# A hybrid decoder layer on one core: parameters loaded as rows of 128 channels, padded sample rows, a first piece split by halves, and matmuls on constants

## The chip, the cores and the metric

The kernel runs on one core of one Trainium2 chip. The metric is the device time of one execution in microseconds; the time before is 1837.62 us, the median of three runs (1835.03 to 1838.05).

## The reference, cut to what matters

One layer of a decoder, for 256 prompt tokens and 8 x 8 sample tokens, D = 2048 channels, all in float32. The part that the change touches is the start:

```
u    = rmsnorm(x, norm_pre_mix)                 # x * rsqrt(mean(x^2) + eps) * w, 320 tokens
proj = u @ w_in                                 # columns: z | xBC | dt | glu
xbc  = silu(conv4(xbc, ssd_conv_w) + ssd_conv_b)
y    = ssd_scan(...) + d_skip * x               # 32 heads
v    = glu_a * sigmoid(glu_b)
vc   = conv31(v, conf_conv_w) + conf_conv_b     # depthwise, over time
conf = silu(layernorm(vc) * conf_norm_w + conf_norm_b)
x    = x + rmsnorm(concat(...) @ w_out, norm_post_mix)
x    = x + rmsnorm(relu(rmsnorm(x, norm_pre_mlp) @ w_up)^2 @ w_down, norm_post_mlp)
```

The per-channel vectors (convolution taps and biases, norm weights, d_skip) come from HBM as rows over 2048 or 3072 channels, and the kernel wants them with the channels on the partitions.

## The kernel before

**Layout.** Activations are held transposed: 16 tiles (NT = 16) of 128 channels by 320 tokens (TOK). A product is exact to about float32 by splitting both sides into a rounded high part (`whi`, `ahi`) and a remainder (`wlo`, `alo`), each as fp32r, and adding three matmuls: hi x hi, hi x lo, lo x hi. Weights come in pieces of 512 channels by 256 columns (512 KB) into four slots `raw[:, slot]`. For each piece ScalarE (ACT) writes `whi` (L662), VectorE (DVE; later in the kernel also GpSimd, POOL) writes `wlo` (L1184, L496), and TensorE (PE) then runs 2 column tiles x 4 channel tiles x 3 = 24 matmuls of 128x128 by 320 columns. Nearly the whole kernel is this stream; every engine's order is written out by hand, and the engines meet only at counting semaphores. A slot is loaded again once its remainder has been taken (`lo_done[slot]`).

**The prologue.** The order of the first 67 us, before the steady stream starts with the loop of L1748 to L1750, is:

1. SyncE (SP) issues the three input loads (`xn`: chunk 2 holds the 64 sample rows, chunks 0 and 1 the 256 prompt rows) and weight pieces s = 0 to 3 (L347), then 14 small loads (L350 to L359) into `prow`, `prow2` and `dsk`: the 31 taps as 31 partitions of 2048 channels, each norm vector and bias as one partition of 2048 channels, the xBC taps and bias as 4 and 1 partitions in two parts. Then pieces s = 4 to 7 and four small pieces s = 8 to 11 (the dt columns), each behind the `lo_done` of its slot. The whole of it is one queue.
2. ACT loads `norm_pre_mix` a second time as one row (`prow0`, L669); PE turns it by 16 transposes of one row (L1757), ACT copies it out as `pmx`.
3. For chunk 2, then 0, then 1: ACT squares and sums the rows (L678) and takes the root (L680), DVE takes the reciprocal (L1199) and scales the rows in place (L1202; chunk 1 in two halves of 1024 columns).
4. PE turns the scaled rows (`turn_rows`, L1763): tiles 0 to 3 ahead of the first piece, in the order chunk 2, chunk 0, tile by tile, then chunk 1. A transpose of chunk 2 loads 64 rows as weights, one of chunks 0 and 1 loads 128. The other twelve tiles are turned one or two at a time between half pieces of matmuls (`TURNS`, `turn_x`), into four PSUM banks that ACT has to empty.
5. ACT rounds piece 0 (`first_split(0)`), then tiles 0 to 3 (`x_hi`, L693), then piece 1, then copies tiles 0 to 3 for later use (`x_keep`, L697); for every later tile it copies and rounds, with the later pieces' `whi` between them. DVE takes piece 0's remainder, the tiles' remainders (`in_lo`, L1208), and so on in the same pattern. Both engines run in order: where ACT waits for piece s to land (`raw_ready`), the tiles behind it wait too.
6. PE's matmuls of a piece (`first_piece`, L1797 to L1799) wait for the whole piece's `lo_done`, and, in the first column tile of every even piece, channel tile by channel tile for `act_ready`. s = 0 to 7 are two column blocks of the glu projection. Then PE turns the parameters (16 transposes of 45 rows at L1812, 8 of 5 rows at L1815), ACT copies them to `par` (channels x parameter) and `sw`, and PE runs the dt pieces s = 8 to 11, twelve matmuls of 32 columns each.
7. Beside it, ACT stores the copied transposed input to HBM (L716, one 2560 KB transfer, once all 16 tiles are copied), and POOL, once PE has used 2, 4 and 6 pieces, loads the convolution states (L454, L457) for use in the stage behind the prologue.

Of the kernel before, what the change touches and what calls it, by code (L numbers as in the profile page):

```python
# [38 lines left out]
TOK = SEQ + NB * DS  # L39
HEADS, HD, GROUPS, STATE = 32, 64, 4, 128  # L40
D_XBC = D + 2 * GROUPS * STATE
# [16 lines left out]

R_CONV, R_CB, R_NW, R_NB, R_SSD, R_PREMIX, R_POSTMIX, R_PREMLP, R_POSTMLP, R_XW, R_XB, R_DSKIP = (
    1, 32, 33, 34, 35, 36, 37, 38, 39, 40, 44, 0)  # L60
NROW = 45

# [42 lines left out]
def build(nc, x_prompt, x_sample, state_ssm, state_ssd_conv, state_conf, w_in, ssd_conv_w, ssd_conv_b,  # L105
# [3 lines left out]
    with ExitStack() as ctx:  # L109
        def sem(name):  # L110
            return ctx.enter_context(nc.semaphore(name))
# [31 lines left out]
        sst = place("sst", [NB * XHALO, D_XBC], at=ar + 15360)  # L143
        prow = place("prow", [NROW, D], at=ar + 18432)
        prow2 = place("prow2", [XTAPS + 1, D_XBC - D], at=ar + 20480)

# [56 lines left out]
        pmx = place("pmx", [P, NT], at=own + 1032)  # L203
        prow0 = place("prow0", [1, D], at=2 * NT * TOK + 4096 * 2 + 2048)
        dsk = place("dsk", [1, HEADS], at=sm)
        hw = place("hw", [HEADS, 8, TOK], at=ar + 18432)
# [26 lines left out]


        raw_ready = [sem(f"raw_ready{s}") for s in range(4)]
        hi_done, weights_used = sem("hi_done"), sem("weights_used")
# [11 lines left out]
        x_trans, x_copied, t1_done = sem("x_trans"), sem("x_copied"), sem("t1_done")  # L248
        par_trans, par_copied, par_done = sem("par_trans"), sem("par_copied"), sem("par_done")
        rooted = sem("rooted")  # L250
# [76 lines left out]
        def _(sp):  # L327
# [10 lines left out]
            for s in range(12):  # L338
                if s < 8:
                    kq, col, width = s // 2, (COL_GLU + D, COL_GLU)[s % 2], 256  # L340
                else:
                    kq, col, width = s - 8, COL_DT, HEADS
                if s == 2:
                    sp.wait_ge(x_in[0], 16)
                if s >= 4:
                    sp.wait_ge(lo_done[s % 4], s // 4)
                sp.dma_start(raw[:, s % 4, :, 0:width], in_k[:, 4 * kq:4 * kq + 4, col:col + width]  # L347
                             ).then_inc(raw_ready[s % 4], 16)
                if s == 3:
                    sp.dma_start(prow[R_CONV:R_CONV + TAPS, :], conf_conv_w[0]).then_inc(par_in, 16)  # L350
                    for r, w in ((R_CB, conf_conv_b), (R_NW, conf_norm_w), (R_NB, conf_norm_b), (R_SSD, ssd_norm_w),
                                 (R_PREMIX, norm_pre_mix), (R_POSTMIX, norm_post_mix), (R_PREMLP, norm_pre_mlp),
                                 (R_POSTMLP, norm_post_mlp)):
                        sp.dma_start(prow[r:r + 1, :], w).then_inc(par_in, 16)
                    sp.dma_start(prow[R_XW:R_XW + XTAPS, :], ssd_conv_w[0, :, 0:D]).then_inc(par_in, 16)
                    sp.dma_start(prow[R_XB:R_XB + 1, :], ssd_conv_b[:, 0:D]).then_inc(par_in, 16)
                    sp.dma_start(dsk[:], d_skip).then_inc(dsk_in, 16)
                    sp.dma_start(prow2[0:XTAPS, :], ssd_conv_w[0, :, D:D_XBC]).then_inc(par_in, 16)
                    sp.dma_start(prow2[XTAPS:XTAPS + 1, :], ssd_conv_b[:, D:D_XBC]).then_inc(par_in, 16)  # L359

# [287 lines left out]
        def _(act):  # L648
# [19 lines left out]

            act.dma_start(prow0[:], norm_pre_mix).then_inc(pmx_in, 16)  # L669
            act.wait_ge(consts, 2)  # L670
# [104 lines left out]
            def glu(i):  # L775
                second = isinstance(i, int) and i == 1
                for c in range(8):
# [14 lines left out]
                    if c == (7 if second else 5):  # L792
# [3 lines left out]
            act.wait_ge(par_trans, 1)  # L796
            act.activation(par[:, 0:8, :], ps[:, 5, 0:8 * NROW].rearrange("p (t r) -> p t r", t=8), ACT.Copy)
            act.activation(par[:, 8:16, :], ps[:, 6, 0:8 * NROW].rearrange("p (t r) -> p t r", t=8), ACT.Copy)
            act.activation(sw[:, NT:NX, :], ps[:, 6, 360:400].rearrange("p (t r) -> p t r", t=8), ACT.Copy
                           ).then_inc(par_copied, 1)  # L800
            first_split(10)
            first_split(11)
            act.wait_ge(par_copied, 1)
            act.activation(sw[:, 0:NT, :], par[:, :, R_XW:R_XB + 1], ACT.Copy).then_inc(par_done, 1)
            ahead(Q_GLU, 0, 6)
# [373 lines left out]
        def _(dve):  # L1179
# [13 lines left out]

            dve.sem_inc(conv_turn, 1)
            dve.wait_ge(consts, 3)
            for r, c in enumerate((2, 0, 1)):
# [4 lines left out]
                for lo, hi in ((0, D),) if r < 2 else ((0, D // 2), (D // 2, D)):  # L1201
                    dve.tensor_scalar(xn[0:n, c, lo:hi], xn[0:n, c, lo:hi], ss[0:n, c:c + 1], None, ALU.mult  # L1202
                                      ).then_inc(xs_done, 1)

# [7 lines left out]
            def first_split(s):  # L1212
                split(s // 4, s % 4, 256 if s < 8 else HEADS)

            dve.wait_ge(pmx_done, 1)
# [10 lines left out]
            dve.tensor_copy(prow[R_DSKIP:R_DSKIP + 1, :].rearrange("a (h p) -> a h p", p=HD),  # L1226
                            dsk[:].unsqueeze(2).to_broadcast([1, HEADS, HD])).then_inc(dsk_done, 1)
            first_split(8)
# [510 lines left out]
        def _(pe):  # L1739
# [15 lines left out]
            pe.wait_ge(pmx_in, 16)  # L1755
            for t in range(NT):
                last = pe.transpose(ps[:, 4, 480 + t:481 + t], prow0[:, t * P:(t + 1) * P], ident[0:1, 0:1])  # L1757
            last.then_inc(pmx_trans, 1)
# [26 lines left out]

            def first_piece(s, kq, bank, tiles, by_tile=False):
                slot = s % 4
                pe.wait_ge(lo_done[slot], s // 4 + 1)
                for n in range(tiles):
                    for k in range(4):  # L1790
                        kk = 4 * kq + k
                        if by_tile and n == 0:
# [7 lines left out]
                    if n == tiles - 1:  # L1800
                        last.then_inc(weights_used, 1)
                    for t in TURNS.get((s, n), ()):
                        turn_x(t)
# [4 lines left out]
            pe.wait_ge(par_in, 16 * 13)  # L1808
            pe.wait_ge(dsk_done, 1)
            pe.wait_ge(ahi_done, NT)  # L1810
            for t in range(NT):
                pe.transpose(ps[:, 5 + t // 8, (t % 8) * NROW:(t % 8 + 1) * NROW], prow[:, t * P:(t + 1) * P],  # L1812
                             ident[0:NROW, 0:NROW])
            for t in range(8):
                last = pe.transpose(ps[:, 6, 360 + 5 * t:365 + 5 * t], prow2[:, t * P:(t + 1) * P],  # L1815
                                    ident[0:XTAPS + 1, 0:XTAPS + 1])
            last.then_inc(par_trans, 1)
            for kq in range(4):
# [425 lines left out]
```

## Time and profile before

| What | Value |
|---|---|
| median of three runs | 1837.62 us |
| the profiled execution | 1837.5 us |
| its span, first to last instruction | 1835.9 us |
| PE busy | 1801.5 us (98%), 12683 instructions |
| DVE busy | 1090.9 us (59%) |
| ACT busy | 769.6 us (42%) |
| POOL busy | 455.2 us (25%) |
| mean granted clock of TensorE | 0.991 of full speed |

Busy shares are means over the whole span. PE is the engine that sets the end; the other engines matter where PE waits for them. In a table of stretches a count in brackets is that of the instruction records in the stretch; some matmul records can be missing, so a count is a lower bound. "PEld" is TensorE's weight load, which runs beside the matmul before it; the distance between the starts of two weight loads shows the pace of PE better than the duration of one matmul, since matmuls overlap.

### The profile page before, as it was taken

How to read it: one execution, taken by the hardware profiler on the slowest of the kernel's cores; microseconds unless marked ns; L12 is line 12 of the kernel's file. 1: busy time of each engine (PE TensorE's matmuls, PEld its weight loads, DVE VectorE, ACT ScalarE, POOL GpSimd, SP SyncE). 2: the span in 40 equal slices, each digit the busy share in tenths (PEclk: the TensorE clock that was granted, in tenths of full speed). 3: DMA queues.
4: the chain of work that ended last, by engine and by line, in shares of the span. 5: the costliest groups of instructions: out<-in, count | busy, mean ns of one | idle time of the engine just before them, and what ended most of it. 6: DMA issues, size and time to landing. Idle time of an engine off the chain costs nothing.

```text
span 1835.9 us, 33891 instructions
## 1 busy us (share of the span) xinstructions
PE 1801.5 (98%) x12683; PEld 1766.1 (96%) x12683; DVE 1090.9 (59%) x1989; ACT 769.6 (42%) x1139; POOL 455.2 (25%) x351
## 2 busy tenths in 40 slices
PE   7999999999999999999899999999999999999998
PEld 6999999999998988899899999999999999999998
DVE  4568887999787677765675433444334443444434
ACT  5443435555355555643353333333324333333332
POOL 1477676776661222222100000000000000000121
PEclk9999999999998999999999999999999999999999
DMA  7665554555554554564345445444444454444442
GB/s 204 192 177 151 162 142 141 152 150 151 152 148 138 169 160 152 163 207 140 115 134 158 145 147 160 151 137 156 153 149 138 143 167 149 137 145 160 153 138 81
DMA packets 286420, 278.33 MB, mean 152 GB/s; under 512 B 11405, under 2 KB 283789, under 8 KB 285412
## 3 DMA queue, kind: packets, MB, share of 16 engines
q1 hardware_dynamic: 247542, 246.56, 44.1%
q10 hardware_dynamic: 37138, 23.08, 4.1%
q0 software_dynamic: 1648, 7.43, 1.3%
q8 instruction: 62, 1.02, 0.2%
q14 instruction: 30, 0.24, 0.0%
HBM read 261.26 MB, written 17.22 MB: 152 GB/s over the span
## 4 chain that ended last, share of the span: by engine, by line
PE 94%; DVE 2%; ACT 2%; DMA 1%; issue 1%; DVEq 0%; ACTq 0%
PE ps L1748 28%; PE ps L1750 28%; PE ps L1749 28%; DMA raw<-in_w_in 1%; PE ps L2065 1%; PE ps L2066 1%; PE ps L2067 1%; PE ps L2026 1%; PE ps L2020 1%; PE ps L1994 1%; PE ps L1971 1%; PE ps L1797 0%; PE ps L2031 0%; PE ps L2029 0%; DVE yo L1732 0%
## 5 line engine op out<-in xcount | busy, mean ns | idle before, releaser
L1748 PE MATMUL ps<-ahi,whi 128*128 128x320 f32 x2304 | 720.2, 313 | 1.9 <-DVE alo L1435 1.9
L1750 PE MATMUL ps<-ahi,wlo 128*128 128x320 f32 x2304 | 713.8, 310 | 0.0
L1749 PE MATMUL ps<-alo,whi 128*128 128x320 f32 x2304 | 713.7, 310 | 0.0
L662 ACT ACTIVATE whi<-raw 128x1024 fp32r<-128x1024 f32 (+1 forms) x468 | 480.2, 1048 | 474.5 <-PE ps L1750 386.8
L1184 DVE TENSOR_TENSOR wlo<-raw,whi 128x1024 fp32r<-128x1024 f32 x347 | 428.6, 1259 | 250.6 <-ACT whi L662 247.3
L1748 PEld LDWEIGHTS ps<-ahi,whi 128*128 128x128 f32 x2304 | 434.4, 189 | 3.9 <-DVE alo L1435 2.2
L1749 PEld LDWEIGHTS ps<-alo,whi 128*128 128x128 f32 x2304 | 434.5, 189 | 0.5
L1750 PEld LDWEIGHTS ps<-ahi,wlo 128*128 128x128 f32 x2304 | 434.2, 188 | 0.0
L1748 PE MATMUL ps<-hhi,whi 128*128 128x320 f32 x1016 | 314.3, 309 | 0.0
L1750 PE MATMUL ps<-hhi,wlo 128*128 128x320 f32 x1016 | 313.9, 309 | 0.0
L1749 PE MATMUL ps<-hlo,whi 128*128 128x320 f32 x1016 | 313.9, 309 | 0.0
L496 POOL TENSOR_TENSOR wlo<-raw,whi 128x1024 fp32r<-128x1024 f32 x121 | 289.5, 2414 | 97.9 <-ACT whi L662 97.5
L1329 DVE SCALAR_TENSOR_TENSOR ps<-vx,par,ps 128x256 f32<-128x256 f32 (+1 forms) x928 | 290.9, 382 | 11.0 <-ACT vx L725 9.9
L633 POOL TENSOR_TENSOR sq<-ya 128x640 f32<-128x640 f32 x7 | 14.7, 2099 | 836.3 <-DVE ya L1696 836.3
L1749 PEld LDWEIGHTS ps<-hlo,whi 128*128 128x128 f32 x1016 | 190.7, 188 | 0.0
L1748 PEld LDWEIGHTS ps<-hhi,whi 128*128 128x128 f32 x1016 | 190.7, 188 | 0.0
L1750 PEld LDWEIGHTS ps<-hhi,wlo 128*128 128x128 f32 x1016 | 190.7, 188 | 0.0
L1086 ACT ACTIVATE hs<-rh 128x640 f32<-128x640 f32 x32 | 23.6, 739 | 205.9 <-DVE rh L1661 205.9
L1661 DVE SCALAR_TENSOR_TENSOR rh<-ps,rb 128x640 f32<-128x640 f32 x32 | 26.4, 824 | 135.2 <-PE ps L1750 135.1
L1696 DVE TENSOR_TENSOR ya<-ps,ya 128x640 f32 (+1 forms) x23 | 19.0, 824 | 111.0 <-PE ps L1750 111.0
L1664 DVE TENSOR_TENSOR hlo<-hs,hhi 128x640 f32 (+1 forms) x32 | 26.4, 825 | 56.7 <-ACT hhi L1088 56.7
L1748 PE MATMUL ps<-ghi,whi 128*128 128x320 f32 x192 | 59.3, 309 | 0.0
(298 smaller groups left out, 1648.9 us busy)
## 6 DMA issues: line engine op xcount, KB each, us to landing
raw<-in_w_in SPq DMA_DIRECT2D x144, 512.0 KB, 3.7
raw<-in_w_up SPq DMA_DIRECT2D x128, 512.0 KB, 4.4
raw<-in_w_down SPq DMA_DIRECT2D x128, 512.0 KB, 4.5
raw<-in_w_out SPq DMA_DIRECT2D x64, 512.0 KB, 3.5
h<-in_state_ssm ACTq DMA_DIRECT2D x16, 512.0 KB, 5.2
out<-hout ACTq DMA_DIRECT2D x16, 512.0 KB, 3.2
x_transposed<-xt ACTq DMA_DIRECT2D x1, 2560.0 KB, 10.5
xr<-x_transposed POOLq DMA_DIRECT2D x1, 2560.0 KB, 9.6
```

The costliest lines, as they stand in the source:

```text
L496: pool.tensor_tensor(wlo[:, kq, :, :], raw[:, kq, :, :], whi[:, kq, :, :].bitcast(F32), ALU.subtract).then_inc(lo_done[kq], 1)
L662: act.activation(whi[:, kq, :, 0:width], raw[:, kq, :, 0:width], ACT.Copy).then_inc(hi_done, 1)
L1086: act.activation(hs[:], rh[:], ACT.Square).then_inc(hs_done, 1)
L1184: dve.tensor_tensor(wlo[:, kq, :, 0:width], raw[:, kq, :, 0:width], whi[:, kq, :, 0:width].bitcast(F32), ALU.subtract).then_inc(lo_done[kq ...
L1329: ins = dve.scalar_tensor_tensor(out=acc[s] if k else src[s], in0=src[s], scalar=par[:, j, R_CONV + k:R_CONV + k + 1], in1=acc[s], op0=ALU ...
L1661: dve.scalar_tensor_tensor(out=rh[:], in0=ps[:, bank:bank + 2, 0:TOK], scalar=0.0, in1=rbb, op0=ALU.max, op1=ALU.mult).then_inc(rh_done, 1)
L1664: dve.tensor_tensor(hlo[:, ds(4 * i + 2 * p, 2), :], hs[:], hhi[:, ds(4 * i + 2 * p, 2), :].bitcast(F32), ALU.subtract).then_inc(hid_ready, 1)
L1696: dve.tensor_tensor(m, gemm_bank(p), m, ALU.add).then_inc(read_dve, 1)
L1748: pe.matmul(out, wh, hi[:, kk, :], start=(kk == 0), stop=False)
L1749: pe.matmul(out, wh, lo[:, kk, :], start=False, stop=False)
L1750: last = pe.matmul(out, wl, hi[:, kk, :], start=False, stop=(kk == NT - 1))
L1971: last = pe.transpose(ps[:, 6 + b // 4, (b % 4) * P:(b % 4 + 1) * P], h0[:, j % 2, b, :], ident[:])
```

## The change

All of it lies in the prologue.

- **Small loads.** Each parameter vector of 2048 channels is loaded as 16 partitions of 128 channels (`pvec`, eight vectors on 128 partitions, d_skip among them), the 31 taps as 4 x 124 rows of 128 channels (`pcv`: 124 partitions, four rows each), the xBC taps and bias as 96 + 24 rows (`pssd`), and `norm_pre_mix` for `pmx` as 16 rows (`pmx0`). Eleven loads instead of 14 behind piece 3. PE turns them with 4 + 1 + 1 transposes, and `pmx0` with one. ACT's three copies write `par` and `sw` with the channel tile running fastest in what they read; the fourth copy goes. `par` has 39 parameters per tile instead of 45.
- **Sample rows padded.** DVE clears partitions 64 to 127 of chunk 2 at the start, and every row transpose loads 128 rows; the 64 more output columns lie in the unused part of the bank (TOK is 320, three chunks of 128 are 384).
- **Chunk 1 scaled in other parts.** 512 columns, 512 columns, and 1024 columns; the last part moves behind the remainders of tiles 0 to 3. PE waits for it ahead of tile 8.
- **Piece 0 split by halves.** ACT rounds channel tiles 0 and 1 of piece 0, then activation tile 0, then channel tiles 2 and 3; DVE takes remainders in the same order; PE waits for the first half at the start and for the second half at the third channel tile.
- **Matmuls on constants.** PE runs `keep_warm(n)`: n matmuls of the bf16 identity with the zeroed `cum3` (320 columns) into bank 3: 20 behind the `pmx` transpose, 8 behind chunk 2's row transposes, 4 behind chunk 0's, 4 behind chunk 1's. The row transposes of tiles 0 to 3 run chunk by chunk.

```diff
-                    sp.dma_start(prow[R_CONV:R_CONV + TAPS, :], conf_conv_w[0]).then_inc(par_in, 16)
-                    for r, w in (... eight vectors ...):
-                        sp.dma_start(prow[r:r + 1, :], w).then_inc(par_in, 16)
...
+                    sp.dma_start(pcv[:], conf_conv_w[0].rearrange("r (t p) -> (r t) p", p=P).rearrange(
+                        "(q a) p -> a q p", a=4 * TAPS)).then_inc(par_in, 16)
+                    sp.dma_start(pssd[0:XTAPS * NX, :], ssd_conv_w[0].rearrange("r (t p) -> (r t) p", p=P)
+                                 ).then_inc(par_in, 16)
...
+                        sp.dma_start(pvec[(r - R_VEC) * NT:(r - R_VEC + 1) * NT, :],
+                                     w.rearrange("o (t p) -> (o t) p", p=P)).then_inc(par_in, 16)
...
+            def first_halves(h):                                   # ACT
+                if h == 0:
+                    act.wait_ge(raw_ready[0], 16)
+                act.activation(whi[:, 0, 2 * h:2 * h + 2, :], raw[:, 0, 2 * h:2 * h + 2, :], ACT.Copy
+                               ).then_inc(first_hi if h == 0 else hi_done, 1)
-            first_split(0)
+            first_halves(0)
             for t in range(4):
                 act.wait_ge(x_trans, t + 1)
                 x_hi(t)
+                if t == 0:
+                    first_halves(1)
...
             dve.wait_ge(pmx_done, 1)                               # DVE
-            first_split(0)
-            for t in range(4):
+            first_halves(0)
+            in_lo(0)
+            first_halves(1)
+            for t in range(1, 4):
                 in_lo(t)
+            scale_rows(P, 1, D // 2, D)
             first_split(1)
...
+            def keep_warm(n):                                      # PE
+                for _ in range(n):
+                    pe.matmul(ps[:, 3, 0:TOK], identb[:], cum3[:], start=True, stop=True)
             def turn_rows(t, c):
-                b, lo = 4 + t % 4, (0, P, SEQ)[c]
-                n = P if c < 2 else NB * DS
-                return pe.transpose(ps[:, b, lo:lo + n], xn[0:n, c, t * P:(t + 1) * P], ident[0:n, 0:n])
+                return pe.transpose(ps[:, 4 + t % 4, c * P:(c + 1) * P], xn[:, c, t * P:(t + 1) * P], ident[:])
...
+            keep_warm(20)
             pe.wait_ge(pmx_done, 1)
-            pe.wait_ge(xs_done, 2)
-            for t in range(4):
-                turn_rows(t, 2)
-                turn_rows(t, 0)
-            pe.wait_ge(xs_done, 3)
+            for c, warm in ((2, 8), (0, 4)):
+                pe.wait_ge(xs_done, 2 if c == 2 else 3)
+                for t in range(4):
+                    turn_rows(t, c)
+                keep_warm(warm)
+            pe.wait_ge(xs_done, 4)
             for t in range(4):
                 turn_rows(t, 1).then_inc(x_trans, 1)
-            pe.wait_ge(xs_done, 4)
+            keep_warm(4)
+            pe.wait_ge(xs_done, 5)
...
-            for t in range(NT):
-                pe.transpose(ps[:, 5 + t // 8, (t % 8) * NROW:(t % 8 + 1) * NROW], prow[:, t * P:(t + 1) * P],
-                             ident[0:NROW, 0:NROW])
...
+            for q in range(4):
+                pe.transpose(ps[:, 5, 4 * TAPS * q:4 * TAPS * (q + 1)], pcv[:, q, :], ident[0:4 * TAPS, 0:4 * TAPS])
+            pe.transpose(ps[:, 6, 0:P], pvec[:], ident[:])
+            pe.transpose(ps[:, 6, P:P + (XTAPS + 1) * NX], pssd[:], ident[0:(XTAPS + 1) * NX, 0:(XTAPS + 1) * NX]
+                         ).then_inc(par_trans, 1)
```

## Rows read from the trace of the kernel before

**Rows 1.** Stretches of PE: stretch, length, busy (records), clock, DMA share, GB/s.
```profile
16.56:24.09 7.53, 7.53 (x33) 1.00 0.55 152
24.09:38.33 14.24, 14.24 (x91) 1.00 0.62 159
38.33:47.28 8.95, 6.49 (x31) 0.81 0.61 134
39.50:41.90 2.40, 0.00 (x0) 1.00 0.97 226
58.60:60.35 1.75, 1.75 (x25) 1.00 0.99 218
60.35:67.43 7.08, 7.08 (x52) 1.00 0.88 262
67.43:1835.90 1768.47, 1747.52 (x12355) 0.99 0.49 149
```

**Rows 2.** The chain that ended last, 38 to 45 us: start, duration, what.
```profile
19.32 19.76 DMA raw<-in_w_in
39.10 1.07 ACT whi L662
...
40.19 1.22 DVE wlo L1184
```

**Rows 3.** Timeline of SyncE's queue: start, duration of the issue.
```profile
9.12 1.60 SPq L350 DMA_DIRECT2D prow<-in_conf_conv_w  x1
...
15.82 32.15 SPq L347 DMA_DIRECT2D raw<-in_w_in  x8
```

**Rows 4.** DMA at 12:14, 24.2:26.8, 48:50 (packets, MB, share); issue at 15.8.
```profile
q1 hardware_dynamic: 696, 0.70, 110.2%
...
q1 hardware_dynamic: 9, 0.07, 6.7%
...
q1 hardware_dynamic: 528, 0.07, 20.9%
...
raw<-in_w_in SPq DMA_DIRECT2D x1, 512.0 KB, 18.3
```

**Rows 5.** Timeline 12 to 17 us, three engines: start, duration, idle before.
```profile
13.18 1.06 ACT L662 ACTIVATE whi<-raw 128x1024 fp32r<-128x1024 f32 x1 [0.17 <-ACT sx L680]
13.24 1.42 DVE L1202 TENSOR_SCALAR xn<-xn,ss 128x1024 f32<-128x1024 f32 x2
14.57 1.22 DVE L1184 TENSOR_TENSOR wlo<-raw,whi 128x1024 fp32r<-128x1024 f32 x1
15.30 1.78 ACT L693 ACTIVATE ahi<-ps,pmx 128x320 fp32r<-128x320 f32 x4 [1.06 <-PE ps L1763]
15.86 1.92 DVE L1208 SCALAR_TENSOR_TENSOR alo<-ps,pmx,ahi 128x320 fp32r<-128x320 f32 x4
16.56 0.60 PE L1797 MATMUL ps<-ahi,whi 128*128 128x320 f32 x1 [0.66 <-DVE alo L1208]
```

**Rows 6.** Timeline of TensorE's weight loads around two groups of transposes.
```profile
30.55 0.29 PEld L1763 LDWEIGHTS ps<-ident,xn 128*128 128x128 f32 x2
...
31.21 0.19 PEld L1797 LDWEIGHTS ps<-ahi,whi 128*128 128x128 f32 x1
...
70.64 0.49 PEld L1828 LDWEIGHTS ps<-ident,cst 120*128 120x128 f32 x4
71.09 0.19 PEld L1748 LDWEIGHTS ps<-ahi,whi 128*128 128x128 f32 x1
```

**Rows 7.** Stretches of PE again: two of equal length.
```profile
18.25:21.66 3.41, 3.41 (x13) 1.00 0.41 108
42.14:45.55 3.41, 3.41 (x13) 0.50 0.69 142
```

**Rows 8.** DMA issues, 0 to 70 us: KB each, median us to landing.
```profile
x_transposed<-xt ACTq DMA_DIRECT2D x1, 2560.0 KB, 10.5
cst<-in_state_conformer_conv POOLq DMA_DIRECT2D x2, 960.0 KB, 9.2
```

More of the change, by code:

```diff
@@ L56 @@
 XNEW = XHALO + NB * XHALO
-R_CONV, R_CB, R_NW, R_NB, R_SSD, R_PREMIX, R_POSTMIX, R_PREMLP, R_POSTMLP, R_XW, R_XB, R_DSKIP = (
-    1, 32, 33, 34, 35, 36, 37, 38, 39, 40, 44, 0)
-NROW = 45
+R_CONV, R_VEC = 0, 31
+R_CB, R_NW, R_NB, R_SSD, R_POSTMIX, R_PREMLP, R_DSKIP, R_POSTMLP = range(31, 39)
+NROW = 39
 Q_DT, Q_GLU, Q_XBC, Q_Z, Q_WC, Q_WS, Q_MLP = 0, 1, 17, 29, 37, 45, 53
@@ L143, in build @@
         sst = place("sst", [NB * XHALO, D_XBC], at=ar + 15360)
-        prow = place("prow", [NROW, D], at=ar + 18432)
-        prow2 = place("prow2", [XTAPS + 1, D_XBC - D], at=ar + 20480)
+        pcv = place("pcv", [4 * TAPS, 4, P], at=ar + 18432)
+        pvec = place("pvec", [P, P], at=ar + 18944)
+        pssd = place("pssd", [(XTAPS + 1) * NX, P], at=ar + 19072)
+        pmx0 = place("pmx0", [NT, P], at=ar + 19200)
+        dsk = place("dsk", [P, 2], at=ar + 19328)
         mix = place("mix", [P, NT, TOK], at=ar)
@@ L232, in build @@
         ps = ctx.enter_context(nc.psum_tensor("ps", [P, 8, 512], F32))
+        first_hi, first_lo = sem("first_hi"), sem("first_lo")
         raw_ready = [sem(f"raw_ready{s}") for s in range(4)]
@@ L248, in build @@
         x_trans, x_copied, t1_done = sem("x_trans"), sem("x_copied"), sem("t1_done")
-        par_trans, par_copied, par_done = sem("par_trans"), sem("par_copied"), sem("par_done")
+        par_trans, par_done = sem("par_trans"), sem("par_done")
         rooted = sem("rooted")
@@ L1194, in _, with scale_rows @@
             dve.sem_inc(conv_turn, 1)
+            dve.memset(xn[NB * DS:P, 2, :], 0.0).then_inc(xs_done, 1)
             dve.wait_ge(consts, 3)
+            def scale_rows(n, c, lo, hi):
+                dve.tensor_scalar(xn[0:n, c, lo:hi], xn[0:n, c, lo:hi], ss[0:n, c:c + 1], None, ALU.mult
+                                  ).then_inc(xs_done, 1)
             for r, c in enumerate((2, 0, 1)):
@@ L1200, in _ @@
                 dve.wait_ge(rx_done, r + 1)
-                for lo, hi in ((0, D),) if r < 2 else ((0, D // 2), (D // 2, D)):
-                    dve.tensor_scalar(xn[0:n, c, lo:hi], xn[0:n, c, lo:hi], ss[0:n, c:c + 1], None, ALU.mult
-                                      ).then_inc(xs_done, 1)
+                if r < 2:
+                    scale_rows(n, c, 0, D)
+                else:
+                    scale_rows(n, c, 0, D // 4)
+                    scale_rows(n, c, D // 4, D // 2)
             def in_lo(t):
@@ L1213, in first_split, with first_halves @@
                 split(s // 4, s % 4, 256 if s < 8 else HEADS)
+            def first_halves(h):
+                dve.wait_ge(*((first_hi, 1) if h == 0 else (hi_done, 1)))
+                dve.tensor_tensor(wlo[:, 0, 2 * h:2 * h + 2, :], raw[:, 0, 2 * h:2 * h + 2, :],
+                                  whi[:, 0, 2 * h:2 * h + 2, :].bitcast(F32), ALU.subtract
+                                  ).then_inc(first_lo if h == 0 else lo_done[0], 1)
             dve.wait_ge(pmx_done, 1)
-            first_split(0)
-            for t in range(4):
+            first_halves(0)
+            in_lo(0)
+            first_halves(1)
+            for t in range(1, 4):
                 in_lo(t)
+            scale_rows(P, 1, D // 2, D)
             first_split(1)
@@ L1787, in first_piece @@
                 slot = s % 4
-                pe.wait_ge(lo_done[slot], s // 4 + 1)
+                if s:
+                    pe.wait_ge(lo_done[slot], s // 4 + 1)
+                else:
+                    pe.wait_ge(first_lo, 1)
                 for n in range(tiles):
                     for k in range(4):
+                        if s == 0 and n == 0 and k == 2:
+                            pe.wait_ge(lo_done[slot], 1)
                         kk = 4 * kq + k
@@ L1802, in first_piece @@
                     for t in TURNS.get((s, n), ()):
+                        if t == 8:
+                            pe.wait_ge(xs_done, 6)
                         turn_x(t)
@@ L1807, in _ @@
                     first_piece(2 * kq + p, kq, 2 * p, 2, by_tile=(p == 0))
-            pe.wait_ge(par_in, 16 * 13)
+            pe.wait_ge(par_in, 16 * 10)
             pe.wait_ge(dsk_done, 1)
             pe.wait_ge(ahi_done, NT)
-            for t in range(NT):
-                pe.transpose(ps[:, 5 + t // 8, (t % 8) * NROW:(t % 8 + 1) * NROW], prow[:, t * P:(t + 1) * P],
-                             ident[0:NROW, 0:NROW])
[L1814 to L1817, printed above, removed]
+            for q in range(4):
[3 more added lines that the diff above has]
+                         ).then_inc(par_trans, 1)
             for kq in range(4):
```

36 lines of the change are left out of this document (16 added, 20 removed).

## The prediction

> **What bounds the kernel now.** The page comes first: TensorE (PE) is busy 98% of the span, so only PE's own work, its gaps and its clock count. The table of stretches says where it is less than full [rows 1]: behind 67.43 us there are 1768.47 us with 20.95 us of gaps in all, and the change touches none of that code. So everything is decided ahead of 67.43 us, and there, in order, by the first matmul's start at 16.56 us [rows 5], by the rate of the first pieces, and by a hole from 39.50 to 41.90 us in which PE does nothing. The chain of waits [rows 2] tells what ended the hole: the sixth weight piece (s = 5) takes 19.76 us from issue to landing, ScalarE rounds it at 39.10, VectorE takes the remainder at 40.19, and only behind these two do the activations of tiles 9 to 11 (already turned) come through the same two in-order engines, which ends the hole at 41.90.
>
> Why is a 512 KB transfer 18 to 20 us on its way? SyncE issues the parameter loads from 9.12 us and the fifth piece behind them at 15.82 [rows 3], which takes 18.3 us [rows 4]. The transfers' own records give it away. From 24.2 to 26.8 us the queue runs 9 packets of 8 KB at 6.7% of sixteen DMA engines: 6.7% x 16 = 1.07, one engine always busy and fifteen idle; a packet is 0.067 x 16 x 2.6 / 9 = 0.31 us. These are the taps' 31 rows and the vectors' single rows, and each piece waits for its share on that engine. 31 + 8 + 1 such packets and parts of others are 40 x 0.31 = 12.4 us of private queue, the shares of two pieces beside it.
>
> For the clock I compare [rows 7]: 18.25 to 21.66 us shows the same 13 matmul records in 3.41 us as 42.14 to 45.55, where the granted clock is 0.50. The first is therefore also the lower level (1.2 GHz), whatever its 1.00 says; PE had before it only short work and a pause. It is 3.41 / 13 = 0.26 us from matmul to matmul there, against 7.08 / 48 = 0.1475 us at 2.4 GHz in the 48 matmuls of the dt pieces [rows 1].
>
> **The change part by part.**
>
> *Earlier start, by halves.* Today the chain is: ScalarE's third root, whi of piece 0 at 13.18 (1.06 us), VectorE's two scalings of 1024 columns from 13.24 (1.42 us together), wlo at 14.57 (1.22), ahi from 15.30, alo from 15.86, first matmul 16.56 [rows 5]. New: scaling of 512 columns ends at about 13.75 (half of a 1024 one is 0.36; with a fixed part 0.5), PE turns the four tiles of chunk 1, the first done at 14.2; ScalarE's half whi (0.53 to 0.65) is done at 13.8, ahi(0) 14.2 to 14.75; VectorE scales the second 512 to 14.1, half wlo to 14.75, alo(0) to 15.3. First matmul 15.4: 1.15 us earlier. But the second half of the split now stands on both engines between tile 0 and tile 1, so alo(1) comes at 16.4, alo(2) 16.85, alo(3) 17.3, and the first half piece ends at 17.8 in 2.4 us instead of 12 x 0.1475 = 1.77: 0.65 given back. The scaling of the other 1024 columns sits on VectorE ahead of piece 1's wlo, which ends at 19.2, as now; PE asks for it at 20.6. The next turn waits for ScalarE's copy behind piece 1's whi (about 17.9), 0.1.
>
> *Warm matmuls.* 20 behind the pmx transpose (3.7 to about 9), 8, 4 and 4 between the row transposes, where PE waits for VectorE's scalings anyway (20 x 0.26 = 5.2 us are over by 9, and the first row transposes can't start before chunk 2 is scaled, at 9.7). If they raise the clock in time, the stretch 16.56 to 24.09 (7.53 us: two half pieces, three turns [rows 1]) shrinks to what the same work takes later. 24.09 to 38.33 is six half pieces and six turns, 14.24 / 6 = 2.37 each, so 1.77 + 0.60; two half pieces and three turns are 5.3: gain 2.2. If not, 0.
>
> *Rows padded to 128.* Three transposes with a 64-row one among them take 30.55 to 31.21 = 0.66 us from weight load to weight load, though four of 120 rows take 70.64 to 71.09 = 0.45 [rows 6]: about 0.10 each once the height stays the same, 0.19 extra at each change. All at 128: 0.36. Gain 0.30 a turn, twelve turns: 3.6. Bounds: -0.6 (64 more columns, 0.05 a turn, and the gap stays) to 3.6. I take 3.6, since rows 6 have equal heights without the gap. The padding's memset is VectorE's first work, ahead of all scalings.
>
> *Parameter rows of 128 channels.* 14 loads become 11. The single vectors become 16 rows of 512 B, the taps 124 partitions x 4 x 512 B, the xBC parameters 96 and 24 rows. No row shows a 512 B packet; the nearest are 1 KB ones, 1.102 x 16 x 2 / 696 = 0.051 us, and 128 B ones, 0.209 x 16 x 2 / 528 = 0.013 us [rows 4]. The taps' 496 packets are then 0.4 us over sixteen engines at the one end and 25 us on a single engine at the other. I take few engines, under 6 us: 124 partitions are near the 128 of the pieces, which fill all sixteen, but like 31 they are no multiple of 16. Piece 4 then lands near 22 us, piece 5 (issued near 19.3) near 24, long before the 33 us at which PE wants them. The hole goes, and the low clock that follows it: 38.33 to 47.28 holds two half pieces and two turns, 4.75 us at the usual rate, and took 8.95 [rows 1]: gain 4.2. What is late next: nothing before 48; ScalarE needs two keeps, two roundings and one or two splits per 4.2 us of PE, some 2.5 us.
>
> The Trainium skill (DMA: Bandwidth & Descriptors, the section on why a DMA increments its semaphore by 16) says that a transfer runs on the largest number of engines up to 16 that divides the slowest dimension of both sides. By that rule the 31 rows go to one engine, which the 6.7% above confirm, but the new 124 partitions only to four, not sixteen: an estimate of 124 packets each, at 0.051 us 6.3 us. No row shows the four; the sum holds with either.
>
> *Parameter transposes.* 24 become 6 of 96 to 128 rows: the 1.75 us of 58.60 to 60.35 become about 1.2 (six x 0.10, three changes of height at 0.19). Gain 0.6. ScalarE's copies move as many numbers as now, beside the dt pieces: 0. pmx: 16 transposes become one, in a gap: 0. The d_skip copy gets short, beside PE: 0.
>
> *What moves with it.* PE reaches the dt pieces near 49.5 instead of 60.35. The store of the transposed input (10.5 us [rows 8]) starts some 10 us earlier, and so do, more or less, the conv states' loads: all keep their distance to PE's use, because each hangs on PE's own counters. The store may now overlap the second state load by 2 to 3 us.
>
> **Sum.** 1.15 - 0.65 - 0.1 + 2.2 + 3.6 + 4.2 + 0.6 = 11.0 us. From this I take 0.8 for the clock: warm bursts of 8, 4 and 4 with pauses for VectorE between them are thin, and if the clock falls again at 13 to 16 us, the first 12 to 16 matmuls cost 0.11 us more each, some 1.5, in about half of the executions. Gain 10.2. The profiled execution took 1837.5 us (span 1835.9 and 1.6 around it), the median shown is 1837.62; so 1837.6 - 10.2 = 1827.4.
>
> **Rivals.**
> (a) *The clock doesn't hold.* For it: in rows 7 the level changes late and after long busy stretches. Against: 5 us of gapless matmuls stand ahead of it. Price: 2.2 of the sum lost, and the transposes of chunks 2 and 0 with their bursts at 1.2 GHz push chunk 1 back by 0.5: 11.0 - 0.8 - 2.2 - 0.5 = 7.5, so 1830.
> (b) *The hole stays*, because the pieces behind the parameter loads are still late, by a remnant on a few engines or by the conv state load (9.2 us for 960 KB) that starts earlier. Gain 11.0 - 4.2 - 0.8 = 6.0, 1831.6. Against: pieces wanted at 33 have 10 us of slack.
> (c) *It is given back later*: the store of 2560 KB and the state load meet the weights of the next stage, and PE waits behind the dt pieces. In the present trace these weights land next to that same store without a PE gap. It would have to cost 10 us: within 0.2%, 1837.
> (d) *Slower*: all 496 packets of the taps on one DMA engine at 0.051 us. Piece 4, issued at 15.8, then lands near 15.8 + 25 + 3 = 44; from about 31 on, each us later is a us of PE. Split at 46.8 instead of the 33.2 at which PE wants it, it costs 13.6, and 1.7 for the low clock behind such a hole: 11.0 - 0.8 - 13.6 - 1.7 = -5.1, 1843. It is slower than before from a landing near 40 on. For: the 31-row load does go to one engine. Against: 128-partition loads don't, and packets of 1 KB behind each other may well be faster than on sixteen busy engines.
> (e) *The padding doesn't do what it says*: the extra 0.19 belongs to the switch between modes, not to the height. 3.6 becomes -0.6: gain 6, 1831.6.
>
> **How the numbers follow.** Main case 0.66 (own range 1825.5 to 1829.5); (a) 0.12; (b) 0.06; (e) 0.06; (c) 0.05; (d) 0.03; 0.02 for something unseen, either side. Later in the kernel the clock falls at a few gaps, and where such a fall begins differs from execution to execution; the three runs lie 3 us apart. So the range is 1824.5 to 1832.5. About 0.2% (3.7 us) can be told from no change: faster 0.90, same 0.06, slower 0.04.
>
> **What would show it.** The first matmul on weights at 15 to 16 us and its neighbours 0.147 us apart; three equal transposes in about 0.36 us between half pieces; no gap of PE near 40 us, pieces 4 and 5 landing within 10 us of issue; the parameter transposes at 47 to 49 us in 1.2 us; gaps behind the dt pieces summing to about the present 21 us. I am wrong if the first pieces run at 0.26, if the 64-row gap survives, if a weight piece still takes over 15 us to land, or if a new gap stands behind 49 us.

## The result, and the profile after

The changed kernel takes 1825.12 us in the median of six runs (1823.92 to 1827.0), the kernel before beside it 1837.66. The ratio is 0.9938, 95% interval 0.9928 to 0.9948: 11.4 us faster, between 9.6 and 13.2 (the medians lie 12.5 apart). One of the six runs of the kernel before took 2197.66 us, and the ratio, which compares fast runs, leaves it out. The forecast was 1827.4 in a range of 1824.5 to 1832.5, faster with 0.90. The time lies in that range, and 0.4 us below the main case's own range.

The profiled execution takes 1823.92 us, span 1822.3. First the stretches of TensorE (columns as in [rows 1]), the same work where the same work can be named:

```profile
15.52:18.05 2.53, 2.18 (x12) 1.00 0.51 143
18.05:30.11 12.06, 12.06 (x90) 1.00 0.71 211
39.50:41.90 2.40, 2.40 (x19) 1.00 0.91 274
48.18:48.88 0.70, 0.70 (x9) 1.00 1.17 385
48.88:55.90 7.02, 7.02 (x52) 1.00 1.01 287
55.90:1822.30 1766.40, 1743.85 (x12356) 0.99 0.49 149
```

The first line is the first half piece: 2.53 us with 0.35 of gap, at full pace. The third is the place of the old hole: full. The steady loop's first matmul starts at 55.88. Before, it was at 67.27; the 67.43 that stands ahead of the result is the end of the last matmul of the dt pieces. What lies behind the loop's start, code that the change doesn't touch, is 2.3 us shorter (1766.5 instead of 1768.8, by the starts of weight loads).

TensorE's timeline of the start (start, duration, operation, count, and in brackets the idle time before it and what ended it); the constants' matmuls are the bf16 ones:

```profile
3.68 5.51 PE L1790 MATMUL ps<-cum,identb 128*128 128x320 bf16 x20
9.87 0.63 PE L1793 MATMUL ps<-ident,xn 128*128 128x128 f32 x4 [0.67 <-DVE xn L1212]
10.33 1.25 PE L1790 MATMUL ps<-cum,identb 128*128 128x320 bf16 x8
12.67 0.71 PE L1790 MATMUL ps<-cum,identb 128*128 128x320 bf16 x4
15.52 0.39 PE L1835 MATMUL ps<-ahi,whi 128*128 128x320 f32 x1 [0.42 <-DVE alo L1229]
16.55 0.42 PE L1835 MATMUL ps<-ahi,whi 128*128 128x320 f32 x1 [0.35 <-DVE alo L1229]
```

The 20 take 5.2 us at 0.26 each, the four behind chunk 0 take 0.71 with the tail: the pace has doubled by then, and the pauses for VectorE between them don't lose it. The weight loads around a turn and around the parameters, against [rows 6]:

```profile
17.91 0.40 PEld L1793 LDWEIGHTS ps<-ident,xn 128*128 128x128 f32 x3
18.27 0.19 PEld L1835 LDWEIGHTS ps<-ahi,whi 128*128 128x128 f32 x1
...
48.16 0.50 PEld L1852 LDWEIGHTS ps<-ident,pcv 124*128 124x128 f32 x4
48.63 0.14 PEld L1853 LDWEIGHTS ps<-ident,pvec 128*128 128x128 f32 x1
48.73 0.14 PEld L1854 LDWEIGHTS ps<-ident,pssd 120*128 120x128 f32 x1
48.85 0.11 PEld L1835 LDWEIGHTS ps<-ahi,whi 128*32 128x32 f32 x1
```

A turn is 18.27 - 17.91 = 0.36 us instead of 0.66. The six parameter transposes take 48.85 - 48.16 = 0.69 us, 0.11 each, although their heights change among 128, 124 and 120.

SyncE's queue (start and duration of the issue; answers to [rows 3]) and what its transfers took (KB each, us to landing; answers to [rows 4, 8]): piece 4, piece 5, piece 7, the store and the state loads.

```profile
9.23 1.74 SPq L352 DMA_DIRECT2D pcv<-in_conf_conv_w  x1
11.01 5.31 SPq L354 DMA_DIRECT2D pssd<-in_ssd_conv_w  x1
...
20.41 18.60 SPq L349 DMA_DIRECT2D raw<-in_w_in  x8
```

```profile
raw<-in_w_in SPq DMA_DIRECT2D x1, 512.0 KB, 5.1
raw<-in_w_in SPq DMA_DIRECT2D x1, 512.0 KB, 4.9
raw<-in_w_in SPq DMA_DIRECT2D x1, 512.0 KB, 10.5
x_transposed<-xt ACTq DMA_DIRECT2D x1, 2560.0 KB, 10.2
cst<-in_state_conformer_conv POOLq DMA_DIRECT2D x2, 960.0 KB, 8.9
```

Pieces 4 and 5 land 5.1 and 4.9 us after their issue, where they took 18.3 and 19.8. Piece 7, issued just ahead of a state load, still takes 10.5. But one small issue holds SyncE for 5.31 us, and piece 4 is issued at 20.4 where it went out at 15.82 before; I had left it at 15.8. It lands at 25.5 and its half pieces are run from 33.2, so nothing of this shows in TensorE.

Where the 11.3 us come from, by the starts of weight loads of the same half pieces in both traces:

```
                                   before          after          gain
first half piece starts            16.53           15.49          1.04
two half pieces, three turns       16.53-24.09     15.49-20.68    2.37
six half pieces, six turns         24.09-38.33     20.68-33.17    1.75
two half pieces, two turns (hole)  38.33-47.28     33.17-37.33    4.79
up to the parameter transposes     47.28-58.65     37.33-48.16    0.54
parameter transposes               58.65-60.35     48.16-48.85    1.01
dt pieces, to the steady loop      60.35-67.12     48.85-55.85   -0.23
```

### The profile page after: what moved, and what is told of

Read it like the earlier page. It is cut to its first block, busy times and chain, and to the rows that moved or that the text cites. A ratio compares the mean times of both kernels' runs of the same rounds, so it can differ in the third digit from the quotient of the medians.

```text
span 1822.3 us, 33899 instructions
## 1 busy us (share of the span) xinstructions
PE 1793.7 (98%) x12686; PEld 1758.8 (97%) x12686; DVE 1088.4 (60%) x1992; ACT 769.9 (42%) x1139; POOL 457.4 (25%) x351
## 3 DMA queue, kind: packets, MB, share of 16 engines
q8 instruction: 62, 1.02, 0.2%
## 4 chain that ended last, share of the span: by engine, by line
PE 95%; DVE 2%; ACT 1%; issue 1%; DMA 0%; SPq 0%; DVEq 0%; ACTq 0%
PE ps L1778 28%; PE ps L1779 28%; PE ps L1780 28%; PE ps L2103 1%; PE ps L2105 1%; PE ps L2104 1%; PE ps L2064 1%; PE ps L2058 1%; PE ps L1835 1%; PE ps L2032 1%; PE ps L1837 1%; PE ps L1836 1%; PE ps L2009 1%; DMA xn<-in_x_prompt 0%; PE ps L2069 0%
## 5 line engine op out<-in xcount | busy, mean ns | idle before, releaser
L1197 DVE TENSOR_TENSOR wlo<-raw,whi 128x1024 fp32r<-128x1024 f32 x346 | 424.1, 1250 | 245.8 <-ACT whi L666 242.7
## 6 DMA issues: line engine op xcount, KB each, us to landing
x_transposed<-xt ACTq DMA_DIRECT2D x1, 2560.0 KB, 10.2
```

The lines of the kernel that those rows point to most:

```text
L1197: dve.tensor_tensor(wlo[:, kq, :, 0:width], raw[:, kq, :, 0:width], whi[:, kq, :, 0:width].bitcast(F32), ALU.subtract).then_inc(lo_done[kq ...
```

## The experiments

Each was timed beside the kernel before, whose median there was 1836.18 us (e1, e2, e4, e5), 1838.27 (e3, e6, e7, e8) or 1835.11 (e10, e11). "dt" and "loop" are the starts of the first weight load of the dt pieces and of the steady loop in the profiled execution; "root" is when VectorE takes up the last root of the norms (the reciprocal), which the input's arrival moves by up to 0.4 us; "rest" is the span behind the loop's start.

```
                    ratio   95% interval      median   root   dt     loop   rest
before                                        1837.66  13.04  60.35  67.12  1768.8
after               0.9938  0.9928 to 0.9948  1825.12  13.16  48.85  55.85  1766.5
e1_no_warm          0.9947  0.9928 to 0.9966  1827.29  13.02  51.24  58.99  1768.3
e2_short_rows       0.9965  0.9951 to 0.9979  1828.90  13.08  52.22  59.22  1768.0
e3_late_params      1.0031  1.0019 to 1.0044  1842.29  12.99  64.84  73.32  1767.1
e4_whole_piece      0.9944  0.9926 to 0.9962  1824.50  13.07  48.82  55.80  1766.8
e5_params_only      0.9981  0.9972 to 0.9991  1832.09  13.17  54.57  62.15  1765.1
e6_one_engine       0.9973  0.9963 to 0.9983  1832.89  13.13  57.19  64.17  1770.8
e7_only_20          0.9957  0.9942 to 0.9972  1830.31  13.08  49.78  56.77  1769.0
e8_later_quarter    0.9941  0.9924 to 0.9957  1825.82  12.87  48.56  55.54  1766.6
e10_pool_halves     0.9951  0.9938 to 0.9965  1826.94  13.30  48.96  55.92  1769.4
e11_changed_again   0.9944  0.9930 to 0.9957  1825.54  13.16  48.85  55.85  1769.4
```

The rest varies by 5.7 us with no relation to the edits, so dt and loop tell kernels apart more finely than the ratios. Each of them is read from one profiled execution; e11 says how well they repeat. By the ratios alone only e2, e3, e5 and e6 are apart from the changed kernel, the intervals of e1, e4, e7, e8 and e10 overlap its own.

**No matmuls on constants.**

```diff
-                for _ in range(n):
+                for _ in range(0):
```

> The changed kernel without any of the matmuls on constants. Measured by where the steady loop's first matmul stands: 67.43 us in the kernel before, 56.0 in the changed one. Theory (the constants raise the clock): the first matmuls on weights stand 0.26 us apart instead of 0.147 until the clock rises, and the loop starts 2.2 us later, 58.2, between 57 and 59. Rival (the clock would have risen anyway, or the row transposes raise it): 56.0.

The first two half pieces with their three turns take 15.50 to 23.07 = 7.57 us instead of 5.19: 2.38 for the clock, as worked out (2.2). With the root made equal (13.02 against 13.16) it is 2.5 up to the dt pieces. The loop starts 3.14 later, though, and the further 0.75 has another cause. TensorE's first matmul of the loop, and GpSimd's first two remainders there:

```profile
59.02 0.39 PE L1778 MATMUL ps<-ahi,whi 128*128 128x320 f32 x1 [0.63 <-POOL wlo L500]
```

```profile
56.49 4.75 POOL L500 TENSOR_TENSOR wlo<-raw,whi 128x1024 fp32r<-128x1024 f32 x2 [1.63 <-ACT whi L666]
```

and in the changed kernel:

```profile
53.31 4.79 POOL L500 TENSOR_TENSOR wlo<-raw,whi 128x1024 fp32r<-128x1024 f32 x2 [2.30 <-ACT whi L666]
```

The first of the two ends half way, at 58.9 here and at 53.31 + 2.4 = 55.7 in the changed kernel, where TensorE's first matmul of the loop is at 55.88; before, it ended at 65.9 for 67.27. So a cover of 1.4 us has shrunk to 0.2. What GpSimd and ScalarE wait for stands ahead of them in the chain that ended last in e1, the weight piece of the next stage:

```profile
44.30 11.02 DMA raw<-in_w_in
```

It is on its way, beside the store of 2560 KB, for 11.0 us here (and in e5), for 10.2 in the changed kernel and for 9.5 before. Why it differs no run isolates.

**Rows of 64 again.**

```diff
-                return pe.transpose(ps[:, 4 + t % 4, c * P:(c + 1) * P], xn[:, c, t * P:(t + 1) * P], ident[:])
+                n = P if c < 2 else NB * DS
+                return pe.transpose(ps[:, 4 + t % 4, c * P:c * P + n], xn[0:n, c, t * P:(t + 1) * P], ident[0:n, 0:n])
```

> The changed kernel with the sample rows' transposes on 64 rows again. Theory (each change of height costs 0.19 us): twelve turns of 0.66 instead of 0.36 us, loop start 59.6, time 3.6 us longer. Rival (the extra belongs to the switch between matmul and transpose): turns stay at 0.3 to 0.36, loop start 55.4 to 56.0.

Weight loads of this kernel: four 64-row transposes in a row, then a turn.

```profile
9.87 0.33 PEld L1794 LDWEIGHTS ps<-ident,xn 64*128 64x128 f32 x4 [1.69 <-issue]
10.27 0.25 PEld L1790 LDWEIGHTS ps<-cum,identb 128*128 128x128 bf16 x3
...
17.82 0.29 PEld L1794 LDWEIGHTS ps<-ident,xn 128*128 128x128 f32 x2
18.28 0.13 PEld L1794 LDWEIGHTS ps<-ident,xn 64*128 64x128 f32 x1 [0.17 <-issue]
18.48 0.19 PEld L1836 LDWEIGHTS ps<-ahi,whi 128*128 128x128 f32 x1
```

The turn is 0.66 again, and the loop starts 3.37 us later, 3.45 with the root made equal: 0.29 for each of twelve turns. The four short ones beside each other take 10.27 - 9.87 = 0.40 with the one change behind them, less than 0.1 each without it. So it is the change from 128 to 64 and back that costs, not the short load.

**Piece 0 in one part.**

```diff
-            first_halves(0)
+            first_split(0)
             for t in range(4):
                 act.wait_ge(x_trans, t + 1)
                 x_hi(t)
-                if t == 0:
-                    first_halves(1)
...
```

> The changed kernel with piece 0 split as a whole again. Theory (the halves only move a wait): first matmul on weights at 16.1 instead of 15.5, but no wait for the second half between tile 0 and tile 1, first half piece ending within 0.2 us of the present 18.05, loop start 56.0 within 0.3. Rival (the halves buy their 0.6 us): loop start 56.6. If the longer pause lets the clock fall, up to 58.

The first weight load is at 16.17 instead of 15.49, and the second half piece's at 18.25 instead of 18.27. The loop starts at 55.80, 55.89 with the root made equal: the split buys nothing. The constants hold the clock here over a pause of 1.2 us ahead of the first matmul on weights: twelve of these, from 16.17 to the turn at 17.89, take 1.72 us.

**The new loads and their transposes alone.** The changed kernel with piece 0 whole, no constants' matmuls and rows of 64; the parts of chunk 1 stay.

> The changed kernel with only the new parameter loads (and chunk 1 scaled in three parts) left: no matmuls on constants, no padding, piece 0 whole. Theory: no hole of PE near 40 us, parameter transposes short: loop start 67.43 - 4.2 - 0.6 = 62.6, within 0.7. Rival (the hole was as much the conv state load's doing): a gap of PE stays, loop start above 65.

The loop starts 4.97 us ahead of before. Stage by stage, by weight loads: 0.26 at the start, 0.06 in the first two half pieces, 4.20 in the two half pieces of the hole (4.75 us instead of 8.95), 0.24 up to the parameter transposes, 1.02 in them, and 0.81 given back behind them. The gap ahead of the loop (61.88 to 62.18) is again GpSimd's remainder. The ratio gives 3.5 us, 1.7 to 5.1.

**The old loads, issued late.** The kernel before, with the 14 loads behind piece 7 instead of piece 3.

```diff
-                if s == 3:
+                if s == 7:
```

> The kernel before, its parameter loads unchanged in form, but issued behind piece 7 instead of piece 3. Theory (the pieces waited behind the 8 KB rows on one DMA engine, in the one queue): pieces 4 to 7 land within 6 us of issue, the hole of 2.4 us goes and the low clock behind it, loop start 67.43 - 4.2 = 63.2; the parameters land near 45 and hold up nothing. Rival (the hole comes from the conv state load or the bandwidth): hole and loop start stay, 67.4.

A clear miss: slower than before. Stretches of TensorE, what it waited for (us in total, times, longest) and the chain that ended last:

```profile
38.33:47.28 8.95, 8.95 (x59) 1.00 0.75 186
54.00:62.10 8.10, 0.10 (x2) 0.75 0.17 41
58.00:68.30 10.30, 6.24 (x37) 0.51 0.48 130
```

```profile
PE ps L1812 <- DMA prow<-in_ssd_conv_b: 8.0, 1, 8.0
```

```profile
30.45 0.26 SPq L358
30.71 0.04 issue
30.75 30.34 DMA prow<-in_ssd_conv_b
```

The hole at 40 is gone, and the pieces land in time. But the last small load, issued at 30.75, lands 30.3 us later, and the parameter transposes wait 8.0 us for it, with the low clock behind. I had counted 13 us of private queue for the one engine. Beside it the store of 2560 KB and two state loads of 960 KB were on their way, and from 50 to 58 us SyncE's queue moved 8 packets (1.1% of sixteen engines) against the store's 40.6%; I take it that their shares on this engine more than doubled the 13, which no run isolates. Order alone moves the hole; the queue on the one engine has to go.

**The taps on one engine.**

```diff
-                    sp.dma_start(pcv[:], conf_conv_w[0].rearrange( ...
+                    for g in range(4):
+                        sp.dma_start(pcv[TAPS * g:TAPS * (g + 1), :, :], conf_conv_w[0].rearrange(
+                            "r (t p) -> (r t) p", p=P).rearrange("(q a) p -> a q p", a=4 * TAPS)[
+                            TAPS * g:TAPS * (g + 1), :, :]).then_inc(par_in, 16)
```

> The changed kernel with the taps loaded by four transfers of 31 partitions instead of one of 124: the same 496 rows of 512 B, all on one DMA engine if a transfer of 31 partitions runs on one. Theory, by the 0.028 us a packet that the changed kernel's records show: 14 us on one engine, from 16 to about 30; piece 4 lands at 31 to 35, PE waits 0 to 3 us for it, loop start 56 to 60. The prediction's rival of 0.051 us a packet: piece 4 at 44, loop start near 70, slower than the kernel before.

SyncE's queue, DMA from 16 to 22 us (packets, MB, share of sixteen engines), and TensorE's waits from 30 to 42:

```profile
9.08 13.00 SPq L353 DMA_DIRECT2D pcv<-in_conf_conv_w  x4
22.12 2.73 SPq L356 DMA_DIRECT2D pssd<-in_ssd_conv_w  x1
...
28.95 19.06 SPq L349 DMA_DIRECT2D raw<-in_w_in  x8
```

```profile
q1 hardware_dynamic: 257, 0.13, 7.2%
```

```profile
PE ps L1837 <- DVE wlo L1199: 4.9, 1, 4.9
```

257 packets of at most 512 B in 6 us are 0.023 us from one to the next, so 496 take 11.6 us, not 25. By the working that gave 0.051 for 1 KB packets, 0.072 x 16 x 6 / 257 = 0.027, about half. 7.2% x 16 = 1.15, so one engine with its packets overlapping shows as 1.15, not as 1. The miss is the second price: the issuing instructions take long. Four issues hold SyncE for 13.0 us and the next for 2.7, and piece 4 goes out at 28.95 and is rounded at 35.9. I take it that an issue doesn't end while the queue of an engine that it needs is full; the trace shows the durations alone. TensorE waits 4.9 us, and the low clock behind the wait (two half pieces and two turns in 7.35 us instead of 4.16) costs 3.2 more: the loop starts at 64.17, 8.3 us later. This is rival (d) of the forecast, with its place right and its price a little over half: it had 13.6 and 1.7.

**Only the first 20 constants' matmuls.**

```diff
-                keep_warm(warm)
...
-            keep_warm(4)
```

> The changed kernel with the first 20 matmuls on constants, without the 8, 4 and 4. Theory (the pause from 9 to 15.5 us, with transposes alone in it, lets the clock fall again): the first matmuls on weights stand 0.26 us apart, loop start 57 to 59, as without any. Rival (once up, the clock holds over the pause): 56.0.

```profile
12.00:18.50 6.50, 5.13 (x18) 0.50 0.83 250
```

The clock is granted by 8.9 us, falls again at 11.8, behind a pause with little more than row transposes in it, and rises at 18.6. The loop starts 0.92 later, 1.0 with the root made equal. So the 8, 4 and 4 are worth 1.0 of the 2.5 that e1 loses with the root made equal, and the first 20 the other 1.5.

**The second 512 columns of chunk 1 behind the remainders**, and **the same with piece 0's remainders on GpSimd.**

```diff
-                    scale_rows(n, c, D // 4, D // 2)
...
+            scale_rows(P, 1, D // 4, D // 2)
             scale_rows(P, 1, D // 2, D)
...
```

```diff
+            for h in range(2):                                     # POOL
+                pool.wait_ge(*((first_hi, 1) if h == 0 else (hi_done, 1)))
+                pool.tensor_tensor(wlo[:, 0, 2 * h:2 * h + 2, :], raw[:, 0, 2 * h:2 * h + 2, :], ... ALU.subtract)
...
-            first_halves(0)                                        # DVE
-            in_lo(0)
-            first_halves(1)
-            for t in range(1, 4):
+            for t in range(4):
...
```

> The changed kernel with the second 512 columns of chunk 1 scaled behind the remainders of tiles 0 to 3 instead of ahead of them. VectorE's chain from chunk 1's reciprocal to the remainder of tile 3 gets 0.35 us shorter and sets the first half piece: first matmul 15.15, loop start 55.6. Rival (ScalarE's chain is as late): unchanged, 56.0. In the device time neither can be told.

> The changed kernel with the second 512 columns scaled behind piece 0's remainders, and these two remainders made on GpSimd instead of VectorE. Theory (what is left at the start is VectorE's chain of scale and two half remainders, and PE in the first half piece waits for nothing else): first matmul on weights at 15.35 us, first half piece ends at 17.5 (18.05 in the changed kernel), steady loop starts at 55.1 (54.8 to 55.4; 55.85 there), 0.7 us gained in the profile, which the device time can hardly tell: ratio 0.9934, within 0.001. Rival: GpSimd takes 1.2 us for a half remainder and PE waits for it as it waited for VectorE, loop at 56 or later, ratio 0.9940.

e8 starts the loop 0.31 us earlier, but its root is 0.29 earlier: nothing gained. e10 starts it 0.07 later with a root 0.14 later: nothing either. Its theory falls, since TensorE waits for more than VectorE's chain. Its rival is right that GpSimd takes long (1.27 us for a half remainder, from 14.15), but the first is done at 15.4, hardly before the `alo` of tile 0 at 15.6 that TensorE needs as well. VectorE's timeline, first of the changed kernel, then of e10:

```profile
13.36 0.88 DVE L1212 TENSOR_SCALAR xn<-xn,ss 128x512 f32<-128x512 f32 x2
14.15 0.68 DVE L1238 TENSOR_TENSOR wlo<-raw,whi 128x512 fp32r<-128x512 f32 x1
14.82 0.55 DVE L1229 SCALAR_TENSOR_TENSOR alo<-ps,pmx,ahi 128x320 fp32r<-128x320 f32 x1
15.34 0.69 DVE L1238 TENSOR_TENSOR wlo<-raw,whi 128x512 fp32r<-128x512 f32 x1
```

```profile
13.50 0.49 DVE L1217 TENSOR_SCALAR xn<-xn,ss 128x512 f32<-128x512 f32 x1
15.05 0.55 DVE L1233 SCALAR_TENSOR_TENSOR alo<-ps,pmx,ahi 128x320 fp32r<-128x320 f32 x1 [1.06 <-ACT ahi L708]
15.91 1.47 DVE L1233 SCALAR_TENSOR_TENSOR alo<-ps,pmx,ahi 128x320 fp32r<-128x320 f32 x3 [0.31 <-ACT ahi L708]
```

With VectorE freed it idles 1.06 us and then 0.31 us for ScalarE's `ahi`. In the changed kernel VectorE looks like the bound because it is never idle; ScalarE, which waits for the first turned tile and rounds two halves and four tiles in one queue, is just as late.

**The changed kernel again.**

> The changed kernel once more, on the same chip as the run beside it. Every theory: ratio 0.9938 within 0.001, steady loop from 55.85, within 0.3. It tells whether the stretches at the low clock behind the prologue, 26.3 us in the profile of the changed kernel against 34.5 before, belong to the kernel (26 again) or to the execution (25 to 37, and the span behind the loop's start between 1765 and 1769).

Loop at 55.85 to the hundredth, the ratio 0.9944 where it was 0.9938, inside its interval. Two stretches of TensorE, here

```profile
633.90:637.20 3.30, 3.30 (x21) 0.50 0.13 45
55.90:1825.20 1769.30, 1746.96 (x12356) 0.99 0.49 149
```

and in the first profile of it

```profile
633.90:637.20 3.30, 3.30 (x31) 1.00 0.14 44
```

The same matmuls run once at the lower level (1.2 GHz) and once at the higher. In all the clock is low for 32.9 us of this execution and for 26.3 of the other, and the rest is 1769.4 against 1766.5 us. So the 2.3 us behind the loop by which the profiles of before and after differ are no more than two executions of one kernel differ by; 11.3 us are the kernel's, and the ratio says 11.4.

## Why the prediction was right

By its own steps, the gain up to the start of the steady loop:

- *Earlier start, by halves.* Forecast 1.15 - 0.65 - 0.1 = 0.4. The start came 1.04 earlier, and the second half of the split was paid between the tiles as foreseen (0.35 of gap in 2.53 us, forecast 2.4). Yet e4 shows that without the split the second half piece starts at the same 18.25: net 0 for the split. The 0.4 came all the same, from elsewhere: with piece 0 whole, e4 and e5 start 0.36 and 0.26 us earlier than before (16.17 and 16.27 against 16.53), both 0.39 with the root made equal. That is owed to the parts of chunk 1, or to the row transposes chunk by chunk, which no run separates. So the number of this step is right by luck: the halves, after which it is named, give nothing.
- *Constants' matmuls.* Forecast 2.2, measured 2.38 (e1), and a further 0.75 that hangs on GpSimd. Rival (a), that the clock doesn't hold, doesn't happen: the pace is full from the first matmul on in both profiles of this kernel, and in those of e2, e4, e6, e8 and e10, which keep all the constants. The 0.8 that I took off was 1.5 in half of the executions: none of these seven shows the fall, and e7, in which it does fall, loses 1.0, not 1.5. Rival (a) also counted the clock twice, the 0.8 and the 2.2.
- *Padding.* Forecast 3.6, measured 3.45 (e2), that is 0.29 a turn for two changes of height, so some 0.15 at each and not 0.19. Rival (e) is excluded by the same run.
- *Loads, and the hole.* Forecast 4.2 for the hole, measured 4.20 (e5): the mechanism and the size are right. That the whole of e5 gives 4.97 for 4.2 + 0.6 = 4.8 is in part luck: 0.7 more than forecast from the transposes and the stretch ahead of them, 0.3 of earlier start, and 0.8 given back behind the dt pieces nearly cancel. Rival (b) is excluded: pieces 4 and 5 land in 5.1 and 4.9 us, and piece 7 in 10.5 without a gap of TensorE. The step "piece 4, issued at 15.8" failed: SyncE stood 5.3 us in an issue. Piece 4 landed at 25.5 instead of near 22, and the 7.6 us from there to 33.2 hid it. I had counted what the packets cost the engines, and nothing for what they cost the queue that issues them.
- *Packets.* I took "few engines, under 6 us" for the taps. The Trainium skill's rule (DMA: Bandwidth & Descriptors, the section on why a DMA increments its semaphore by 16) gives one engine for 31 partitions; the trace agrees, 7.2% of sixteen in e6 with the new rows and 6.7% in [rows 4] with the old. For the 124 partitions it gives four. The changed kernel shows this:

```profile
q1 hardware_dynamic: 88, 0.05, 31.1%
```

  from 16.5 to 17.0 us, as the first packets behind the weight pieces run. That is 5.0 engines by the share; but e6 shows one engine as 1.15, and its 43 packets per us, against 88 in 0.5 us here, make 4.1 engines. The trace agrees with four, neither one nor sixteen. All small packets are through by 22 us.
- *Parameter transposes.* Forecast 1.2, measured 0.69. I had charged three changes of height at 0.19. The extra time of [rows 6] shows between 128 and 64 rows; among 128, 124 and 120 there is none.
- *Moved work.* "All keep their distance": the store and the states take what they took, 10.2 and 8.9 us against 10.5 and 9.2 in [rows 8]. But the weights behind the store do not keep theirs: they take 10.2 us instead of 9.5 to land and reach TensorE with 0.2 us to spare instead of 1.4 (the dt line of the table above gives 0.23 back), and in e1 and e5 TensorE idles 0.63 and 0.30 us for them. So the mechanism of rival (c) exists, at under 1 us where it would have needed 10.
- *Sum.* 11.0 before the 0.8 was taken off, 11.3 measured. The time itself, 1825.1 against 1827.4, is further off than that: 0.8 is the deduction, 0.3 is what 11.3 exceeds 11.0 by, and the rest is how executions scatter: the medians are 12.5 us apart, the ratio says 11.4 (the six of this kernel from 1823.9 to 1827.0, the five of e11 from 1822.5 to 1828.8).

Put together, up to the start of the dt pieces, ahead of GpSimd's wait: e1, e2 and e5 give 2.39 + 3.37 + 5.78 = 11.5, and the whole change 60.35 - 48.85 = 11.5. The parts add up. Behind that point the stretch to the loop is 6.77 us before, 7.00 in the changed kernel and 7.75 and 7.58 in e1 and e5.

What stays open: what holds SyncE in the long issues, why the weights behind the store take 9.5, 10.2 or 11.0 us, and what the parts of chunk 1 and the new order of the row transposes give each by itself.

## What to carry to other kernels

Here a small parameter load whose partitions didn't spread over the DMA engines delayed the later transfers that had a share on its engine (18 to 20 us instead of 5), and the queue that issued it as well (e6); look at the DMA share in a quiet stretch and multiply by sixteen, and read the duration of the issues beside it. Moving such a load only moved the wait (e3): change its shape. Transposes between matmuls are worth keeping at one height of the loaded operand (0.3 us a turn here), and an engine that is never idle is not shown to be the bound until it has been relieved (e10).

## What the runs showed of the hardware that I had not expected

- An issue is not free: 5.31 us for the 48 KB of the xBC taps right behind the taps' load, 13.0 us for the four of e6, against 0.42 us for each of the 8 KB loads that follow.
- The change from weight loads of 128 rows to 64 and back costs about 0.3 us in a turn, and 128, 124 and 120 beside each other cost nothing over 0.11 us each.
- Packets of 512 B behind each other on one engine follow at 0.023 us (e6), where I expected 1 KB packets at 0.051 to be the nearest case.
- 36 matmuls of a zeroed operand in bf16 bring the clock up (0.26 us apart at first, 0.13 from the second group on) and hold it over pauses of 0.5 to 0.7 us between the groups, in e4 over 1.2 us. The first 20 alone bring it up and don't hold it (e7).
